# Six U slots and six V slots in place of four and eight, with V picks four steps later

## What is computed

```python
for l in range(DEPTH):
    mod = cs @ w_ada[l] + b_ada[l]
    sh1, sc1, gt1, sh2, sc2, gt2 = [m[:, None, :] for m in jnp.split(mod, 6, axis=-1)]
    h = x * (1.0 + sc1) + sh1
    proj = h @ w_in[l]
    ...
    mix = jnp.concatenate([o_mla, o_conv, o_swa], axis=-1) @ w_o[l]
    x = layer_norm(DN_ALPHA * x + (1.0 + gt1) * mix, g_ln1[l], b_ln1[l])
    h = x * (1.0 + sc2) + sh2
    y = peer(h, w_pq[l], sub_keys[l], u_tab[l], v_tab[l])
    x = layer_norm(DN_ALPHA * x + (1.0 + gt2) * y, g_ln2[l], b_ln2[l])

# in peer, for a block of 128 tokens, with experts e and gates g of all heads:
a = jax.nn.gelu(jnp.einsum('bqd,bqkd->bqk', xb, u_tab[e]), approximate=False)
return jnp.einsum('bqk,bqkd->bqd', g * a, v_tab[e])
```

## Time and profile before

| | |
|---|---|
| Median of 3 runs | 1927.07 us (1925.3 to 1928.72) |
| The profiled execution | 1929.44 us |
| Its span, first to last instruction | 1927.6 us |
| Granted TensorE clock, mean | 0.812 |
| PE / DVE / ACT / POOL busy | 68% / 53% / 22% / 50% |
| Bytes moved | 667.14 MB, mean 346 GB/s |

### The profile page before, as it was taken

The page is one execution under the profiler, slowest core; times in us unless marked ns, Lnnn a source line. Parts: engine busy times, 40 slices in busy tenths (PEclk is TensorE's granted clock), DMA queues, the critical chain, the costliest instruction groups (busy, mean ns, idle before and its releaser), DMA issues.

```text
span 1927.6 us, 16473 instructions
## 1 busy us (share of the span) xinstructions
PE 1308.3 (68%) x5162; PEld 574.9 (30%) x5162; DVE 1023.8 (53%) x3010; ACT 420.3 (22%) x1009; POOL 971.0 (50%) x1028
## 2 busy tenths in 40 slices
PE   6886478877666576886675567897765565556445
PEld 2554223543222122353221222354321221111111
DVE  0012755566634337556563556566576666666642
ACT  1543013431210013253030112353120020000100
POOL 0000555446544336645654555554666656666663
PEclk9988598978888787988877778897887777777768
DMA  9826999879999979989999998987999989999996
GB/s 352 318 66 226 338 359 404 290 272 364 399 389 384 382 285 373 402 317 336 388 399 404 365 384 326 404 332 257 388 358 407 369 315 377 384 384 386 350 368 242
DMA packets 218746, 667.14 MB, mean 346 GB/s; under 512 B 22724, under 2 KB 52132, under 8 KB 218660
## 3 DMA queue, kind: packets, MB, share of 16 engines
q0 software_dynamic: 147456, 536.94, 73.0%
q1 hardware_dynamic: 71204, 129.16, 18.4%
HBM read 664.97 MB, written 1.05 MB: 346 GB/s over the span
## 4 chain that ended last, share of the span: by engine, by line
PE 25%; DMA 25%; DVE 14%; issue 13%; POOL 11%; another core or an unknown queue 8%; ACT 4%; SPq 1%; POOLq 0%; DVEq 0%; ACTq 0%
DMA ring<-in_u_tab,uidx 14%; PE y L1592 7%; DVE ring L1153 7%; DMA wo<-in_w_ada 7%; POOL ring L590 5%; POOL ring L578 5%; DMA ring<-in_v_tab,vidx 3%; PE m L1369 3%; PE m L1259 2%; PE m L1261 2%; PE qb L1542 2%; PE m L1484 2%; PE m L1454 1%; PE m L1305 1%
## 5 line engine op out<-in xcount | busy, mean ns | idle before, releaser
L578 POOL DMA_INDIRECT ring<-in_u_tab,uidx x512 | 484.1, 945 | 710.0 <-DVE ring L1153 382.0
L1153 DVE SCALAR_TENSOR_TENSOR ring<-ring,hp 128x1024 f32<-128x1024 f32 x512 | 618.9, 1216 | 387.1 <-DMA ring<-in_u_tab,uidx 306.1
L1592 PE MATMUL y<-ring,place 128*32 128x512 f32 x2048 | 596.8, 751 | 284.2 <-DMA ring<-in_v_tab,vidx 163.3
L590 POOL DMA_INDIRECT ring<-in_v_tab,vidx x512 | 486.8, 951 | 224.9 <-issue 152.6
L1592 PEld LDWEIGHTS y<-ring,place 128*32 128x32 f32 x2048 | 122.6, 125 | 577.9 <-issue 575.0
L1542 PE MATMUL qb<-wpq,hT 128*128 128x256 f32 x512 | 144.6, 415 | 14.1 <-DVE vidx L1174 10.8
L1542 PEld LDWEIGHTS qb<-wpq,hT 128*128 128x128 f32 x512 | 94.9, 200 | 102.4 <-issue 93.0
L925 DVE TENSOR_TENSOR modc<-m,colT 128x4 f32<-128x4 f32 x24 | 3.9, 162 | 190.6 <-PE m L1271 187.0
L1305 PE MATMUL m<-win,hT 128*128 128x480 f32 x192 | 91.3, 622 | 8.4 <-ACT hT L652 3.6
L722 ACT ACTIVATE cdiag<-cst,wdT 128x128 f32<-128x128 f32 x248 | 78.9, 392 | 49.1 <-PE m L1369 35.0
L1580 PE MATMUL qb<-cst,spread_coef 128*128 128x16 f32 x64 | 16.8, 341 | 105.3 <-DVE spread_coef L1166 55.1
(11 more groups left out here) (220 smaller groups left out, 1398.2 us busy)
## 6 DMA issues: line engine op xcount, KB each, us to landing
wo<-in_w_ada SPq DMA_DIRECT2D x30, 1024.0 KB
wpq<-in_w_pq SPq DMA_DIRECT2D x28, 1024.0 KB
win<-in_w_in SPq DMA_DIRECT2D x32, 720.0 KB, 18.4
ring<-in_w_ada SPq DMA_DIRECT2D x18, 1024.0 KB, 8.9
wo<-in_w_o SPq DMA_DIRECT2D x32, 512.0 KB
ring<-in_u_tab,uidx POOLq DMA_INDIRECT x512
ring<-in_v_tab,vidx POOLq DMA_INDIRECT x512
small<-in_w_uq SPq DMA_DIRECT2D x2, 768.0 KB
```

The costliest lines, as they stand in the source:

```text
L578: nc.gpsimd.indirect_dma_start(out=ring[:, n % UR, :], out_offset=None, in_=u_flat, in_offset=bass.IndirectOffsetOnAxis(ap=uidx[:, g % 2, ...
L590: nc.gpsimd.indirect_dma_start(out=ring[:, UR + n % VR, :], out_offset=None, in_=v_flat, in_offset=bass.IndirectOffsetOnAxis(ap=vidx[:, g ...
L1153: v.scalar_tensor_tensor(ring[:, n % UR, :], ring[:, n % UR, :], 1.0, HP[:, :], ALU.mult, ALU.mult, accum_out=dots[:, g % 2, k:k + 1]).the ...
L1592: e = mm(Y[n][lo:lo + QUAD, :], place[:, g % 2, run_of(k), :], ring[:, UR + k % VR, n * 512:(n + 1) * 512], start=False, stop=False, tile_ ...
```

## The change

`UR` goes from 4 to 6 and `VR` from 8 to 6; the ring has twelve slots as before. A constant `LAG` of 4 is added. POOL issues the V gather of pick n - 4 (not n) after the U gather of pick n + 16, and PE weighs pick n - 4 at step n, so PE's loop runs four steps longer and the sums of a block are cleared and closed four steps later. PE turns the coefficients at step 2 of a turn (before: ahead of step 0). DVE copies the V indices at step 1 (before: 2) and makes `place` at step 3 (before: 2). The query work of PE and ACT lies one step later. All that follows the end of a block's turns (mixing of blocks 2 and 3, second norms, gates, two chunks of the modulation, the stores) lies four steps later. No instruction is added or removed but the order and the waits.

```diff
-UR = 4
-VR = 8
+UR = 6
+VR = 6
+LAG = 4
...
-BASE = (-140, 0, PH * TOPK, 2 * PH * TOPK)
+BASE = (-140, 0, PH * TOPK + LAG, 2 * PH * TOPK + LAG)
...
-        return 85 + 4.2 * c if c < 10 else (214, 225)[c - 10]
+        return 85 + 4.2 * c if c < 10 else (218, 229)[c - 10]
...
-    return (m + 1) * PH * TOPK - (1 if m < BLOCKS - 1 else 20)
+    return (m + 1) * PH * TOPK + (LAG - 1 if m < BLOCKS - 1 else -20)
...
-                    yield LAST_SLOT if t else (BLOCKS - 1) * P + 10
+                    yield LAST_SLOT + LAG if t else (BLOCKS - 1) * P + LAG + 10
...
-            for i in range(-1, TURNS):
-                for k in range(TOPK):
-                    if i + 1 < TURNS:
-                        gather_u(i + 1, k)
-                    if i >= 0:
-                        gather_v(i, k)
+            for n in range(-TOPK, TURNS * TOPK + LAG):
+                if n + TOPK < TURNS * TOPK:
+                    gather_u(*divmod(n + TOPK, TOPK))
+                if n >= LAG:
+                    gather_v(*divmod(n - LAG, TOPK))
...
-                        if k == 8:
+                        if k == 9:
                             query_out(i + 3)
-                        if k == 10:
+                        if k == 11:
                             turned_query_out(i + 3)
-                        if k == 12:
+                        if k == 13:
                             scores_out(i + 3)
...
+                    if k == 1 and 0 <= i + 1 < TURNS:
+                        turn_indices(i + 1)
                     if k == 1 and i >= 0:
                         coefficients(i)
-                    if k == 2 and i >= 0:
+                    if k == 3 and i >= 0:
                         placements(i)
-                    if k == 2 and 0 <= i + 1 < TURNS:
-                        turn_indices(i + 1)
...
-                pe.wait_ge(s["vidx_ready"], g + 1)
+                pe.wait_ge(s["vidx_ready"], min(g + 2, TURNS))
...
-            for i in range(-3, TURNS):
+            for i in range(-3, TURNS + 1):
                 if i >= 0 and (i + 1) % PH == 0 and i + 1 < TURNS:
                     block_rows((i + 1) // PH)
-                if i >= 0:
-                    if i % PH == 0:
-                        clear_sums(i // PH)
-                    turn_coef(i)
-                for k in range(TOPK):
-                    if i >= 0 and k % 2:
-                        weigh(i, (k - 1, k))
+                for k in range(TOPK if i < TURNS else LAG):
+                    g, p = divmod(i * TOPK + k - LAG, TOPK)
+                    if g >= 0 and g % PH == 0 and p == 0:
+                        clear_sums(g // PH)
+                    if k == 2 and 0 <= i < TURNS:
+                        turn_coef(i)
+                    if g >= 0 and p % 2:
+                        weigh(g, (p - 1, p))
                     if i + 3 < TURNS:
-                        if 4 <= k < 8:
-                            query_products(i + 3, range(2 * k - 8, 2 * k - 6))
-                        if k == 9:
+                        if 5 <= k < 9:
+                            query_products(i + 3, range(2 * k - 10, 2 * k - 8))
+                        if k == 10:
                             query_transposes(i + 3)
-                        if k == 11:
+                        if k == 12:
                             query_scores(i + 3)
```

More of the change, by code:

```diff
@@ L563, in _ @@
                                  output_weights(3, BASE[3] + 30, ("ad", 1, ADA_CHUNKS - 1)), stores())
-            upto(LAST_SLOT)
+            upto(LAST_SLOT + LAG)
             sp.wait_ge(s["out_stored"], 16 * TB)
@@ L871, in _ @@
                                  second_norm(0, BASE[2]), mixing(2, BASE[2]), second_norm(1, BASE[3]), mixing(3, BASE[3]),
-                                 second_norm(2, (BLOCKS - 1) * P), second_norm(3, LAST_SLOT))
+                                 second_norm(2, (BLOCKS - 1) * P + LAG), second_norm(3, LAST_SLOT + LAG))
             for i in range(-3, TURNS):
@@ L1585, in weigh @@
                 for k in ks:
-                    pe.wait_ge(v_in[k % VR], 16 * ((g * TOPK + k) // VR + 1))
+                    n = g * TOPK + k
+                    pe.wait_ge(v_in[n % VR], 16 * (n // VR + 1))
                 if ks[0] == 0:
@@ L1592, in weigh @@
                         e = mm(Y[n][lo:lo + QUAD, :], place[:, g % 2, run_of(k), :],
-                               ring[:, UR + k % VR, n * 512:(n + 1) * 512],
+                               ring[:, UR + (g * TOPK + k) % VR, n * 512:(n + 1) * 512],
                                start=False, stop=False, tile_position=(0, lo))
@@ L1640, in _ @@
                         turn_index(i + 2)
-                if i >= 0 and i % PH == PH - 1:
-                    close_sums()
+                    if g >= 0 and g % PH == PH - 1 and p == TOPK - 1:
+                        close_sums()
 def shape_constants(np):
```

## The result

The changed kernel takes 1872.78 us (median of four runs, 1861.81 to 1875.43), the kernel before 1927.02 (1925.3 to 1928.72) beside it. By these medians 54 us are saved (0.9719), where the prediction had 22. The ratio as estimated from all the runs is 0.9691, 95% interval 0.9649 to 0.9734. The direction and the range held; the amount is two and a half times the forecast. The profiled run took 1871.94 us.

The account below looks back on a forecast made before the run. About half the turns were held full by DMA engines, the others by POOL's waits, mostly for four U slots. Start 5, stalls 33, quiet turns 5, lag 9, less 30 for V slots: 22 us saved, 1927 to 1905, range 1868 to 1955.

Parts of the forecast that it names:

- Start (a): First turn's 16 U gathers, 35.5 us: six U slots in place of four save 5 us, bounds 0 and 8.5.
- Stalls (b): Nine turns with a stall: three more gathers, 3.7 us, fill each; 33 us saved, bounds 11 and 45.
- Quiet turns (c): Eight turns like 1652:1697.8, at most 2 us each from more U slots: 5 us saved, bounds 0 and 16.
- The sentence on the Trainium skill: With about 358 GB/s as a core's HBM limit, full turns give nothing and the time is 1910 us.
- The lag: Turn starts: V pairs no longer stand in slots while coefficients are made; 9 us saved, bounds 0 and 25.
- Two fewer V slots: POOL is stopped two pairs earlier where PE is late: six times 5.0 us, 30 us lost, bounds 0 and 105.
- The end: After the last U gather, four more V gathers are covered by the wait for `place`: zero, bounds -5 and 5.
- Moved steps: Queries, indices, `placements` and work after a block's turns come later: zero; about 3 us per block if cover is gone.
- V slots bind: Rival, 0.30: PE late by more than 3.3 us where DMA engines aren't full, 15 such spells; slower, 1950 us.
- Stalls filled wholly: Rival, 0.17: PE is rarely late once its turns start without a wait; 72 us saved, 1855 us.
- The DMA engines take it back: Rival, 0.11: gathers issued sooner in a poor turn only queue in the full one behind it; 1925 us.
- No effect: Rival, 0.02: the change doesn't do what it says; 1927 us.

Follow-up runs that it names:

- before_again: The kernel before, unchanged, run again on a faster chip: 1855.81 us, ratio 0.9997.
- u4v8_lag4: The changed kernel with four U and eight V slots, so the lag and the moved steps alone: 1822.75 us, ratio 0.9818 to the kernel before.
- after_again: The changed kernel, unchanged, run again on a faster chip: 1809.31 us, ratio 0.9736 to the kernel before.
- u6v6_tail: The changed kernel with the V gathers of picks 502 to 507 put into U slots: 1864.86 us, ratio 0.9647 to the kernel before.

## Why the prediction was right and wrong

**Right: what bounds the kernel.** The poor turns with mixing and the start carry the gain, the quiet ones hardly change (45.8 to 44.9 us in the turn of the earlier trace rows; 399.1 to 395.9 for nine of them in the table), and the gathers' queue went from 73.0 to 74.4% of the DMA engines' time.

**Start (a), 5 us in bounds of 0 to 8.5: too small, but within its bounds.** Turn 0 went from 35.5 to 27.3 us, 8.2. The prediction held that DVE, busy for 24.5 us of it, would stop it near 30; DVE was busy for 22.2 of the 27.3 and did not. In the table turns 0 and 1 together give 6.9 us by the lag and 10.1 by the slots; the second turn was no term of the sum.

**Stalls (b), 33 us: the right place, but too large for the slots.** In the table the nine mixing turns give 25.0 us, of which 10.4 are the slots' and 14.6 the lag's; that is net of the V slots' price there, which was a term of its own. The prediction's own nine turns, counted by POOL's U gathers in the same traces, take 480.2, 458.1 and 448.4 us: 22.1 by the lag and 9.7 by the slots. In the stall that answers to the earlier trace rows POOL issues five gathers after PE's L1456 has started at 1286.63, before it waits (timeline: start, us, what, idle before it):

```profile
1286.63 3.79 PE L1456 MATMUL m<-vrows,win 128*128 128x64 f32 x32
...
1286.93 0.94 POOL L581 DMA_INDIRECT ring<-in_u_tab,uidx  x1 [0.30 <-issue]
...
1292.08 0.93 POOL L581 DMA_INDIRECT ring<-in_u_tab,uidx  x1 [0.30 <-issue]
...
1295.42 0.69 DVE L1061 TENSOR_TENSOR h<-m,rinv 128x512 f32<-128x512 f32 x1 [10.53 <-remote]
...
1300.94 0.94 POOL L593 DMA_INDIRECT ring<-in_v_tab,vidx  x1 [7.93 <-PE y L1595]
```

DVE's wait is nearly as long as it was (10.53 us, 11.51 before), POOL's is 7.93 in place of 13.73. It now ends with a V slot that PE frees, as the prediction's text said of L1454. But the two stalls are not alike in PE, and the 5.8 us between them are not the slots' alone. Before, the granted clock was 0.50 there, the lower of its two levels, after PE had been idle for 3.44 us, and L1454 took 7.06 and 3.62 us; after, it was 1.00 and the first part took 3.79 us:

```profile
1332.00:1342.60 10.60, 10.52 (x49) 10.55 (x50) 0.70 (x2) 1.53 (x3) 0.49 (x1) 0.50 0.31 117
```

```profile
1286.60:1290.50 3.90, 3.90 (x36) 3.87 (x35) 0.00 (x0) 0.37 (x1) 2.82 (x4) 1.00 1.01 368
```

On the faster chips this stall is at a clock of 1.00 already before, and POOL's wait behind it is shorter from the start (before_again, u4v8_lag4, after_again):

```profile
1304.04 0.94 POOL L578 DMA_INDIRECT ring<-in_u_tab,uidx  x1 [6.90 <-DVE ring L1153]
```

```profile
1281.72 0.94 POOL L581 DMA_INDIRECT ring<-in_u_tab,uidx  x1 [2.76 <-DVE ring L1155]
```

```profile
1268.08 0.94 POOL L593 DMA_INDIRECT ring<-in_v_tab,vidx  x1 [1.67 <-PE y L1595]
```

So the row on which term (b) was built, 13.73 us, was taken at the lower clock. At the higher one there is less to win: the lag alone takes 4.1 of the 6.9 us, and six and six without the lag leave POOL no stop there at all (idle times of 0.30 us).

**Quiet turns (c), 5 us: right in size** (3.2 us in nine quiet turns of the table, 2.4 of them by the slots; on the slower chip the two kernels differ there by 12.1 us, 427.3 to 415.2, counted by products and by 2.5 counted by U gathers, so the size isn't fixed better than that). The 10.2 us for four U slots of the earlier trace rows had looked like the bound, but with six slots the turn is hardly shorter, and its DMA share is 1.01 after 1.00.

The sentence on the Trainium skill can be closed: by its figure of about 358 GB/s (DMA: Bandwidth & Descriptors, Specifications) the full turns had nothing to give. The turns here reach 404 GB/s after the change (304.1:357.7) and 409 GB/s in a stretch of before_again,

```profile
1699.00:1748.00 49.00, 28.93 (x110) 9.81 (x102) 36.38 (x111) 5.98 (x11) 35.38 (x37) 0.81 1.03 409
```

so the measurement decides against it as a limit of this core. The same page of the Trainium skill (Bandwidth, Measured) has about 425 GB/s for a core that streams alone, which no run here contradicts.

**The lag, 9 us in bounds of 0 to 25: the step that failed.** Alone it saves 1.8% of 1854.64, 34 us (32 by the medians), beyond my upper bound. The prediction reasoned that PE's waits reach POOL as waits for V slots, and so put them within the 72 us of the earlier trace rows. The runs show another way. With four and eight slots the lag took next to nothing from POOL's waits for V slots (16.5 to 12.9 us): of the 30 us that went from POOL's idle time 28 stood ahead of U gathers, as waits for DVE. Behind PE's waits in its queue stand the query and mixing steps, and DVE needs the results of mixing before it goes on with products, which free the U slots. The traces bear this out. From the first U gather to the last, DVE's waits for PE, all their rows added, are 189.3 us in before_again and 155.8 with the lag alone, those for ACT 26.3 and 14.8. With six and six slots and no lag they are 191.7 and 27.1, so it is the lag that does it. The largest of these rows, in before_again and in u4v8_lag4:

```profile
DVE modc L925 <- PE m L1271: 113.3, 14, 20.8
```

```profile
DVE modc L927 <- PE m L1273: 95.8, 12, 17.7
```

That the gain is in the start, the mixing and the `w_ada` turns (37 us) and not in quiet ones (1) agrees with this. I had named that queue ("with queries and mixing queued behind it") and then priced only the V side. Which of PE's two waits matters is shown in part: at four and eight slots the wait for `place`, put back by halving the lag, costs about 1% of the 1.8 (0.9918 against 0.9818), the wait for `spread_coef`, put back, nothing that the runs can tell (0.9834). The other 0.8% lies in the first half of the lag and the moved steps, and stays open.

**Two fewer V slots, 30 us in bounds of 0 to 105: not one number.** By the run it is 5 us with four U slots. With six, a seventh V slot is worth 10 to 12 us (0.9691 to 0.9627, and 0.9647 to 0.9594), so two may be worth some 20, nearer to the 30 that I took; six and eight wasn't run. Both figures compare different chips and hold the cut of `DIAGS`. Without the lag the loss eats the whole gain of the U slots and 8 us more. The prediction set each term against the kernel before and added; here the terms depend on each other. The net of the slots was 13 us by the sum (5 + 33 + 5 - 30). Measured it is 15 to 24 with the lag (0.9818 to 0.9736 or 0.9691), and a loss of 8 without. The forecast's 22 and the 54 thus differ by the lag above all (9 against 34).

**The end, 0 in bounds of -5 to 5: wrong, -10 to -14.** The cover that I named holds: the last `place` still comes 14.3 us after the last U gather.

```profile
1811.25 0.94 POOL L581 DMA_INDIRECT ring<-in_u_tab,uidx  x1 [0.31 <-issue]
...
1824.64 0.94 POOL L593 DMA_INDIRECT ring<-in_v_tab,vidx  x1 [3.74 <-PE y L1595]
...
1825.51 0.88 DVE L1183 TENSOR_TENSOR place<-cst,qb 128x128 f32<-128x128 f32 x4 [5.64 <-PE qb L1582]
...
1848.41 0.94 POOL L593 DMA_INDIRECT ring<-in_v_tab,vidx  x1 [0.30 <-issue]
```

But in those 14.3 us POOL may issue only what fits in V slots, and the four older picks take them first (21 gathers follow the last U gather, 17 before; I had counted 20 and 16, the same four more). Fifteen of the last gathers follow `place`, ten before. I counted gathers by POOL's 1.24 us and forgot that they need slots. By run: 39.8 us from last product to end before, 42.0 with the slots alone, 43.4 with the lag alone, 54.2 with both, so this loss too is made by the pair. Six more slots for the last gathers (u6v6_tail) gave back some 4 us of it.

**Moved steps, 0: nothing against it.** DVE waits once for `sc`, 15.7 us, where it waited twice for 16.3 in all; the queries at their old picks bring no gain (0.9756).

**The rivals.** "V slots bind" was right as a mechanism: the idle time ahead of V gathers rose by 282 us. It was to decide if that were more than the fall ahead of U gathers, and that fell by 336. So my own sign for it says no, as does the quiet turn of 44.9 us, under 48. "Stalls filled wholly" had 1855, and its prices for the lag and the V slots (15 and -5) were nearer to the truth than mine, those for stalls and quiet turns (45 and 12) further off. Its cause isn't there: PE's part in POOL's waits has grown, not vanished. "The DMA engines take it back" may be seen in places, in turn 10 (50.1 to 54.0 us) and turns 7 and 8 (14.4 more, counted by U gathers). It isn't shown: turn 10 went from 50.6 to 47.6 us by the same count in before_again and after_again. In the table turns 7 and 8 shorten by the lag alone (162.3 to 147.1), and the slots give back 9.5 of it (156.6). That may be the V slots beside SP's loads, or what the slots issue sooner; the runs don't tell these apart. "No effect" is out.

**By the signs given.** Wait for L1153 under 250 us: 35.7. Stall with POOL idle for some 10 us: 7.93. PE's waits nearly gone: 67.3 to 14.0 for `place`, but 55.1 to 34.6 for `spread_coef`, half right. The faster chip, whose traces lack no releaser, has 71.1 to none and 119.3 to 23.1. First turn some 30 us: 27.3.

## What to carry to other kernels

When two rings share one in-order queue, a slot moved from one to the other may only move the wait: here six and six gave nothing until the lag came with it, so test such edits alone and together, and don't add their terms. When a wait of an engine is removed, price what is queued behind it and follow that to the bound, not only the buffers that the engine frees. And count the drain by slots as well as by instructions: a lag that costs nothing in the middle can cost its length at the end.

## What the runs showed of the hardware

The same program has a pace that depends on the chip: the kernel before took 1854.64 and 1855.6 us on two chips and 1930.54 and 1930.05 on two others. The granted clock of the profiled runs differs a little (0.812 and 0.830). One more difference is in the idle time before ACT's copies of PE's results, and in what ended it. On the chip of the first profile:

```profile
L849 ACT COPY sc<-qb 128x256 f32<-128x256 f32 x32 | 11.9, 372 | 162.4 <-remote 74.0 <-PE qb L1561 54.2 <-issue 34.2
```

In before_again, of the same code on a faster chip, and one such copy there from the timeline:

```profile
L849 ACT COPY sc<-qb 128x256 f32<-128x256 f32 x32 | 11.9, 372 | 128.4 <-PE qb L1561 128.4
```

```profile
1722.60 1.23 PE L1561 MATMUL qb<-skT,qT 128*128 128x128 f32 x4
1723.86 0.37 ACT L849 COPY sc<-qb 128x256 f32<-128x256 f32 x1 [6.45 <-PE qb L1561]
```

On the faster chip ACT starts 0.03 us after the matmul's end as recorded, and no wait lacks a releaser. On the slower one the copy of the earlier trace rows starts 13.4 us after it. Of the 977 updates of PE's semaphores in that trace, 66 come 6 to 20 us after the start of the last matmul recorded for them; in before_again it is 2 of 1206. The slower chip's trace thus also holds 229 fewer updates, so some of its waits without a releaser may be gaps in the record. All ten traces from chips on which the kernel before takes some 1930 us have such waits ahead of V gathers (44.1 to 92.5 us), none of the eight from the faster chips has. The prediction took this lateness for a trait of the kernel and built the V slots' price on it. It goes with the chip, and the changed kernel's ratio is no worse where it occurs (0.9691 against 0.9736). How much of the 4% it makes, whether the updates are late or the records incomplete, and why on some chips alone, stays open.
